# Three edits to the order of work in a two-block transformer kernel: block copies ahead of exponentials, scores ahead of the second turn, and bounded decays in the state-space stage

## The reference, cut to what matters

```
# SSD, per chunk of 128 tokens and per head
seg    = a_cum[l] - a_cum[s]
decay  = exp(where(causal, seg, -inf))           # causal: s <= l
cb     = einsum('bclgn,bcsgn->bclsg', Cc, Bc)
y_diag = einsum('bclsgj,bcsgjp->bclgjp', cb[..., None] * decay, X)

# windowed attention (layers 0 and 3), and MLA (layer 1, no sink, all keys)
m = maximum(max(logits), sink); e = exp(logits - m)
p = e / (sum(e) + exp(sink - m)); o = p @ v
```

## Time and profile before

| | |
|---|---|
| median of 3 runs | 3486.39 us |
| the profiled execution's own time | 3492.03 us |
| its span | 3490.2 us |
| granted TensorE clock, mean | 0.924 of full |
| PE / DVE / ACT busy | 84% / 52% / 33% of the span |
| chain that ended last | PE 65%, DVE 23%, ACT 6%, issue 4% |

### The profile page before, as it was taken

One profiled execution on the slowest core, in us unless ns is written; L12 is line 12 of the kernel. 1 busy time (PEld: TensorE's weight loads), 2 busy tenths in 40 slices (PEclk: granted clock), 3 DMA queues, 4 the chain that ended last, 5 costly groups with the idle time before them and its releaser, 6 DMA issues.

```text
span 3490.2 us, 39924 instructions
## 1 busy us (share of the span) xinstructions
PE 2937.7 (84%) x16196; PEld 2362.7 (68%) x16196; DVE 1832.2 (52%) x3328; ACT 1166.1 (33%) x1970; POOL 746.9 (21%) x160
## 2 busy tenths in 40 slices
PE   4966977787989999989888796898899777579886
PEld 2845855665777788769665585667699766458665
DVE  5784454553632999920576501444810477561473
ACT  3323333332213122242465424442422200342462
POOL 2401412221333444413001131002123100013101
PEclk7988988898999999999999998999999877799998
DMA  6303421221232555321001111002112200312101
GB/s 258 141 13 126 181 85 49 109 109 37 85 121 106 205 194 191 148 85 61 25 2 49 73 61 49 1 1 85 73 61 97 85 1 1 121 73 85 37 2 61
DMA packets 49174, 291.64 MB, mean 84 GB/s; under 512 B 4320, under 2 KB 5600, under 8 KB 19424
## 3 DMA queue, kind: packets, MB, share of 16 engines
q1 hardware_dynamic: 22464, 163.59, 12.9%
q10 hardware_dynamic: 26528, 125.50, 9.4%
HBM read 268.10 MB, written 20.97 MB: 83 GB/s over the span
## 4 chain that ended last, share of the span: by engine, by line
PE 65%; DVE 23%; ACT 6%; issue 4%; DMA 1%; ACTq 0%; DVEq 0%; PEldq 0%
PE psum L413 17%; PE psum L414 17%; PE psum L415 17%; DVE ada_temp L714 3%; PE psum L1483 2%; DVE pair_row L1542 2%; PE psum L1479 1%; PE psum L1308 1%; PE psum L1491 1%; PE psum L862 1%; PE psum L1502 1%; PE psum L2526 1%; DVE pair_prob L1553 1%; ACT pair_prob_t L1582 1%; DVE h L885 1%
## 5 line engine op out<-in xcount | busy, mean ns | idle before, releaser
L400 POOL TENSOR_TENSOR w_lo<-raw,w_hi 128x2048 fp32r<-128x2048 f32 x156 | 746.7, 4787 | 2701.3 <-ACT w_hi L408 2701.3
L413 PE MATMUL psum<-a_hi,w_hi 128*128 128x512 f32 (+3 forms) x1880 | 705.1, 375 | 101.1 <-DVE a_lo L871 66.0
L414 PE MATMUL psum<-a_lo,w_hi 128*128 128x512 f32 (+3 forms) x1880 | 699.5, 372 | 0.0
L415 PE MATMUL psum<-a_hi,w_lo 128*128 128x512 f32 (+3 forms) x1880 | 698.3, 371 | 0.0
L714 DVE SCALAR_TENSOR_TENSOR ada_temp<-ada_ring,ada_rows 128x1024 f32<-128x1024 f32 x240 | 434.9, 1868 | 120.9 <-DMA ada_ring<-ada 56.0
L413 PEld LDWEIGHTS psum<-a_hi,w_hi 128*128 128x128 f32 (+1 forms) x1880 | 357.3, 190 | 184.3 <-issue 72.7
L415 PEld LDWEIGHTS psum<-a_hi,w_lo 128*128 128x128 f32 (+1 forms) x1880 | 357.5, 190 | 63.0 <-issue 2.0
L414 PEld LDWEIGHTS psum<-a_lo,w_hi 128*128 128x128 f32 (+1 forms) x1880 | 358.2, 191 | 58.5 <-issue 0.3
L408 ACT ACTIVATE w_hi<-raw 128x2048 fp32r<-128x2048 f32 x156 | 298.0, 1911 | 257.0 <-DMA raw<-stream 117.5
L414 PE MATMUL psum<-w_lo,a_hi 128*128 128x256 f32 x800 | 226.4, 283 | 0.0
L415 PE MATMUL psum<-w_hi,a_lo 128*128 128x256 f32 x800 | 226.4, 283 | 0.0
(11 more groups left out here) (388 smaller groups left out, 4792.0 us busy)
## 6 DMA issues: line engine op xcount, KB each, us to landing
raw<-stream SPq DMA_DIRECT2D x156, 1024.0 KB, 4.8
ada_ring<-ada ACTq DMA_DIRECT2D x72, 1024.0 KB, 5.9
xres<-x_in ACTq DMA_DIRECT2D x4, 3072.0 KB, 10.1
x_in<-xres ACTq DMA_DIRECT2D x3, 3072.0 KB, 10.1
gates<-gate_part ACTq DMA_DIRECT2D x8, 768.0 KB, 3.8
c_z<-gates ACTq DMA_DIRECT2D x1, 3072.0 KB, 16.7
c_og<-gates ACTq DMA_DIRECT2D x1, 2304.0 KB, 9.7
x<-xT ACTq DMA_DIRECT2D x1, 2048.0 KB, 9.5
```

What stands on the lines that cost most here:

```text
L400: pool.tensor_tensor(k.w_lo[:, r], k.raw[:, r], k.w_hi[:, r].bitcast(F32), ALU.subtract) \
L413: pe.matmul(out, lhs[0], rhs[0], start=start, stop=False)
L414: pe.matmul(out, lhs[0], rhs[1], start=False, stop=False)
L415: return pe.matmul(out, lhs[1], rhs[0], start=False, stop=stop)
```

## The change

In `pair_attention`, ScalarE's order in iteration p becomes copy 2p-2, exps 2p, copy 2p-1, exps 2p+1, take p-2. TensorE issues `scores(0)` ahead of the loop, and then in iteration p: turn 2p-2, values p-2, scores p+1, turn 2p-1 (in MLA with values 2p-4 ahead of all this and values 2p-3 behind turn 2p-2). VectorE's order stays. All three attention stages use this function.

In the SSD stage the two chained additions become one minimum of the row with the token's own a_cum; -a_cum is added as the bias of the exponential, which is why ScalarE now makes four exponentials 128 wide in place of one 512 wide; and the causal zeros come from multiplying `cb` once for each of the two groups by the triangle of ones and zeros.

```
-            k.dve_chain(dve, dve.tensor_copy(cb[:, g, :], k.psum[:, 6 + g, :]))
-        tri = k.cst("tri").unsqueeze(1).broadcast_to([P, 4, P])
-        mask = k.cst("mask_le").unsqueeze(1).broadcast_to([P, 4, P])
+            k.dve_chain(dve, dve.tensor_tensor(cs(cb[:, g, :]), cs(k.psum[:, 6 + g, :]), tri, ALU.mult))
...
-            nac = c4(nacum)[:, :, h:h + 1].broadcast_to([P, 4, P])
-            k.dve_chain(dve, dve.tensor_tensor(cs(seg[:, h % 3]), cs(k.psum[:, h % 2, :]), mask, ALU.add))
-            dve.tensor_tensor(cs(seg[:, h % 3]), cs(seg[:, h % 3]), nac, ALU.add).then_inc(seg_ready.sem, 1)
+            start = c4(acum)[:, :, h:h + 1].broadcast_to([P, 4, P])
+            dve.tensor_tensor(cs(seg[:, h % 3]), cs(k.psum[:, h % 2, :]), start, ALU.min) \
+                .then_inc(seg_ready.sem, 1)
...
-            act.activation(seg[:, h % 3], seg[:, h % 3], ACT.Exp)
+            for c in range(4):
+                decay = seg[:, h % 3, c * P:(c + 1) * P]
+                act.activation(decay, decay, ACT.Exp, bias=c4(nacum)[:, c, h:h + 1])
...
+        scores(0)
         for p in range(n + 2):
-            if p < n:
-                scores(p)
-            if halves:
-                if 1 <= p <= n:
-                    turn(2 * p - 2)
-                if p >= 2:
-                    values(p - 2, (2 * p - 4, 2 * p - 3))
-                if 1 <= p <= n:
-                    turn(2 * p - 1)
-            else:
-                if 2 <= p:
-                    values(p - 2, (2 * p - 4,))
-                if 1 <= p <= n:
-                    turn(2 * p - 2)
-                if 2 <= p:
-                    values(p - 2, (2 * p - 3,))
-                if 1 <= p <= n:
-                    turn(2 * p - 1)
+            if 2 <= p and not halves:
+                values(p - 2, (2 * p - 4,))
+            if 1 <= p <= n:
+                turn(2 * p - 2)
+            if 2 <= p:
+                values(p - 2, (2 * p - 4, 2 * p - 3) if halves else (2 * p - 3,))
+            if p + 1 < n:
+                scores(p + 1)
+            if 1 <= p <= n:
+                turn(2 * p - 1)
...
         for p in range(n + 2):
+            if 1 <= p <= n:
+                copy(2 * p - 2)
             if p < n:
                 exps(2 * p)
             if 1 <= p <= n:
-                copy(2 * p - 2)
+                copy(2 * p - 1)
             if p < n:
                 exps(2 * p + 1)
-            if 1 <= p <= n:
-                copy(2 * p - 1)
             if p >= 2:
                 take(p - 2)
```

More of the change, by code:

```diff
@@ L1119, in _ @@
     def _(dve):
+        tri = k.cst("tri").unsqueeze(1).broadcast_to([P, 4, P])
         for g in range(2):
-            k.dve_chain(dve, dve.tensor_copy(cb[:, g, :], k.psum[:, 6 + g, :]))
-        tri = k.cst("tri").unsqueeze(1).broadcast_to([P, 4, P])
-        mask = k.cst("mask_le").unsqueeze(1).broadcast_to([P, 4, P])
+            k.dve_chain(dve, dve.tensor_tensor(cs(cb[:, g, :]), cs(k.psum[:, 6 + g, :]), tri, ALU.mult))
         def rows(h):
```

## The result

The changed kernel takes 3714.98 us (median of 4 runs, 3713.83 to 3722.81), the kernel before 3486.42 us in the same comparison (4 runs, 3484.45 to 3488.73): a ratio of 1.0656 [1.0642, 1.067], 228.5 us more. The profiled execution has a span of 3721.0 us against 3490.2, and a mean granted clock of 0.898 of full against 0.924.

A forecast was written before the change was run, and what follows sets the result against it. Bounds: a loop through three engines in layer 0's attention, TensorE in MLA, VectorE in the SSD decays. Terms 109 + 16 + 30 - 10 + 38 = +183 gave a median of 3669 us, range 3618 to 3742.

The forecast's parts named there:

- closed ring: Attention stages: both new orders together make a pair's steps wait in sequence, 6.09 us a wide pair against 4.38.
- clock term: Wide pairs of layers 0 and 3: TensorE's clock falls in three of ten pairs, at 2.0 us each, +38 us.
- rival with a low clock throughout the wide pairs: Layers 0 and 3: TensorE's clock stays low through all wide pairs, 3727 to 3791 us; chance 0.15.
- six steps: Attention: masks done, next scores, second turn, its copy, next second exponential, scaling, next masks; 6.56 us for a 640-wide pair.
- Either edit alone leaves the ring open: Attention: TensorE's or ScalarE's new order alone does not close the loop, only the two together; no size given.
- Wide pairs +109: Layers 0 and 3: 64 wide pairs each take 1.71 us longer through the closed loop, +109 us.
- Context pairs +16: Context pairs: 16 pairs of 256 columns take 3.7 us against 2.71 through the loop, +16 us.
- the clock's bounds: Wide pairs of layers 0 and 3: from none of 64 at the lower clock (0) to all (+96 to +160 us).
- MLA +30: MLA: a group of six pairs takes 50.4 us against 43.0, +7.4 for each of four groups, +30 us.
- SSD -10: SSD decays: VectorE loses an addition and a chain wait per head, four short exponentials hidden; -10 us, bounds -11 and -4.
- rival with a full clock: Attention stages: the loop closes but TensorE's clock stays full, +145 with the SSD gain, 3631 us; chance 0.28.
- signs that I named: Profile after: L1135 gone, exponentials behind waiting copies, reciprocal idle about 3 us, wide pairs 6.1 us apart, stage times.

The follow-up runs named there:

- e5: Changed kernel with ScalarE's second exponential of a pair moved back ahead of the second copy, TensorE's new list kept: 3479.23 us, ratio 0.9959 to the kernel before.
- e4: Changed kernel with one or two extra unread matmuls a pair behind the second turn in layers 0 and 3: 3649.73 us, ratio 1.0454 to the kernel before.
- e7: Changed kernel with extra unread matmuls behind the second turn in layers 0 and 3 and in MLA too: 3641.04 us, ratio 1.0425 to the kernel before.

## Why the prediction was right, and where its sizes were off

The kind and the place were right: slower by a closed ring, 228.5 us where 183 was forecast, inside the range (3714.98 us in 3618 to 3742). The 45.5 us between them are mostly a clock term that was half of what it should be. In total the time is nearer to the rival with a low clock throughout the wide pairs (3727 and more) than to the forecast of 3669, but not by that rival's way, since half of the wide pairs kept the full clock. By its steps:

- *The ring, step by step.* Shown. The changed timeline has the six steps in the order given, and moving one copy (e5) removes the loss. 6.16 us a wide pair with the clock held, for 6.09 forecast.
- *Either edit alone leaves the ring open.* Right for TensorE's (ratio 0.9986). For ScalarE's I overlooked that the turn still stands behind the values; that edit alone costs 0.7%, part of it by the clock in the context pairs. All edits together, the SSD edits with their gain among them, cost far more than the sum of both.
- *Wide pairs +109, and their share of the clock term, +38.* Measured 76.1 + 75.5 = 151.6 for 147. The clock's part by e4 is 42.1. That this is near 38 is luck. I took three pairs in ten at 2.0 us, 0.6 us a pair, without a row for the three; the trace has every second pair at 1.16 or 1.54 us, which is 0.68 a pair. The price was made up wrongly too: I had +1.05 for scores and +0.45 for the turn, and the long pair at 1784.94 has its scores near the full clock and pays in the turn (1.33 for 0.77) and in the values (1.97 for 1.09). TensorE's idle time itself was right: 2.11 to 2.39 us for 2.0 to 2.25.
- *Context pairs +16.* Measured +35.4. With the clock held (e7) they cost 58.7 - 42.5 = 16.2, as forecast. The missing 19.1 is the clock: my term was for the 64 wide pairs, and I named the context pairs only as pairs that had never fallen. **This is the term that was mis-sized most**, since the clock's bounds spoke of 64 pairs and left 16 out.
- *MLA +30.* Measured +40.2; 33.8 with the clock held, and 6.4 of clock for which the sum had no term; the one window of MLA that I had read kept 1.00 with little work.
- *SSD -10.* Measured -10.3, and -10.4 alone. The four short exponentials are hidden, as assumed; they last 1.28 us together, start to end, within the 0.7 to 2.0 that I had bounded, for the 1.0 taken. By the Trainium skill ("ScalarE: Activation LUTs", rules for kernel authors) my estimate was 1.6 us; the trace has less because back to back each starts 0.30 us after the one before (1.28 less 0.386, over three), though it lasts 0.386.
- *Outside the stages.* +13.9, which no term had. In e7 it is -2.2, but that holds -5.1 from the stretch between SSD and layer 0, where no edit reaches and the profiles scatter from 1417.1 to 1423.4 us. The 4.4, 4.1 and 2.8 us behind the attention stages are 3.3, 0.7 and -0.8 there, so the clock may be the cause behind MLA and layer 3, and the rest stays open.
- *The clock in all.* The forecast had 38. Held up (e7) the loss is 149, where the rival with a full clock said 145; without it 228.5. So the clock costs some 80 us. The Trainium skill ("Perfetto Trace Analysis", Matmul Optimizations) said that matmuls should run in batches without gaps; e4 agrees plainly, with 20 us for each set of wide pairs won by work of no use.

Of the signs that I named, these came: the addition of L1135 gone, copies that wait for their turn in every unit, and pairs at 6.1 to 6.25 us at the full clock. The reciprocal's wait was put near 3 us. In the wide pairs of layer 0 it is 3.0 with the clock held (94.4 over 31 in e4) and 3.8 in the changed kernel (117.8 over 31); the mean of 4.1 over all stages (409.5 over 101) comes from MLA, which has 6.1 (127.2 over 21). Layer 3's window of 223.8 is near the 225 given, MLA's 219.0 is above the 208, and layer 0 has 217.8 + 78.5 for 290.

What stays open: the reason for the 9.8 us that ScalarE's order alone costs in wide pairs is read from their timeline and not tested by a run, and the two attention edits without the SSD edits were not run together.

## What to carry to other kernels

With hand-ordered lists, follow a new order from one event until it comes back to the same event, through all engines, before judging either list: two edits that cost -0.1% and +0.7% alone made the kernel 6.6% slower together, with the SSD edits' gain of 0.4% already in it. An instruction whose input is ready should not stand behind one that waits for another engine; here the place of a single copy was worth about 7% of the time (1.0656 against 0.9959). And when a loop gets longer, ask in each stage what TensorE's clock does in the new idle time; the shortest stage lost the largest share to it here (19.1 us in 16 pairs).

## What the runs showed of the hardware that was not expected

The lower level of TensorE's clock can last through a stretch in which TensorE is busy for a larger share than in stretches that keep the full clock. (A matmul at the lower level takes longer, so a larger share is not more work: 18 matmuls in 4 us below, where the stretch at the full clock has 247 in 40.) In the kernel before, context pairs ran at the full clock with TensorE busy for 29.96 of 40 us:

```profile
1840.00:1880.00 40.00, 29.96 (x247) 16.86 (x244) 30.49 (x144) 27.86 (x102) 0.00 (x0) 1.00 0.01 2
```

With ScalarE's order alone these pairs ran at the full clock too from 1852 us on (0.67 in the window before), 2.97 us apart. Then came idle times of 1.40 and 0.88 us, the clock fell, and it stayed there for the rest of the stage, with TensorE busy for 3.60 of every 4 us (TensorE's timeline, then its own windows of 4 us):

```profile
1862.45 0.44 PE L1491 MATMUL psum<-const,pair_prob 128*128 128x128 f32 x2 [1.40 <-DVE pair_prob L1553]
1862.81 0.66 PE L1502 MATMUL psum<-pair_prob_t,gv 128*64 128x128 f32 x8
...
1865.41 0.69 PE L1491 MATMUL psum<-const,pair_prob 128*128 128x128 f32 x2 [0.88 <-DVE pair_prob L1553]
```
```profile
1860.00:1864.00 4.00, 2.60 (x22) 1.00 0.00 0
...
1868.00:1872.00 4.00, 3.60 (x18) 0.50 0.00 0
...
1900.00:1904.00 4.00, 3.60 (x18) 0.50 0.00 0
```

The same happened in the changed kernel: its context pairs began with the clock between both levels (0.61 and 0.82 in the windows from 1908 and 1912 us), and from 1916 us on every window has 0.50. In the wide pairs the clock came back each time, there behind an unbroken run of work (1784.94 to 1788.17 in the timeline above: turn and values without idle time, and then the scores near the full clock); a context pair has a break in every period, of 0.40 us in the one kernel and 1.55 in the other. Nor does the length of the idle time alone tell what comes: behind 2.22 and 2.29 us the clock fell, and behind 2.11 and 2.39 us, in the pairs between, it did not. So one fall costs about one long pair where wide pairs follow, and the rest of the stage where context pairs follow. That the unbroken run is what brings it back was not tested. With idle time that can't be taken away, matmuls whose results nobody reads can be worth their time, as e4 and e7 show.
